# A mixture-of-experts stage whose tiles are weighted at the gate and added in DRAM by an accumulating indirect transfer

## The chip, the cores and the metric

The kernel runs on one core of one Trainium2 chip. The metric is the device time of one execution in microseconds (us), median over runs. A core has five engines with instruction streams of their own: TensorE (PE in the profile; its weight loads are PEld), VectorE (DVE), ScalarE (ACT), GpSimd (POOL) and SyncE (SP, which here only issues transfers). 16 DMA engines carry the transfers that SP, ACT and POOL issue.

## The reference

One layer of a decoder over 2048 prompt tokens and 64 sample tokens (8 x 8), 1024 channels: adaLN modulation, a state-space branch beside windowed attention, an output projection with residual (x2), and a mixture of experts. The part that is changed:

```python
def hier_moe(x, ...):          # top-1 of 4 groups, then top-2 of its 4 experts
    wts = g_p * top_p / jnp.sum(top_p, axis=-1, keepdims=True)
    eid = g_idx[:, None] * EXPERTS_PER_GROUP + top_i
    gates = jnp.sum(jax.nn.one_hot(eid, N_EXPERTS) * wts[..., None], axis=1)
    hg, hu = einsum('td,edf->tef', xt, w_gate), einsum('td,edf->tef', xt, w_up)
    act = jax.nn.silu(hg) * hu * gates[..., None]
    return jnp.einsum('tef,efd->td', act, w_down)
...
ffn = hier_moe(hn2, ...)       # hn2: normed and modulated x2
x = x + gt2 * rms_norm(ffn, p['g_post_ffn'])
```

So each token has two experts, each with a weight; the two weighted outputs are summed, the sum is normed, and x2 is added. An expert has gate and up weights of 1024x256 each and down weights of 256x1024, in fp32. Products are computed in fp32 accuracy as three products of rounded and residual halves.

## The kernel before

The stages run one after the other: front, state space, attention, mixing, experts. The change touches the last two.

**Mixing** (function mixing) goes over 17 tiles of 128 tokens (NT = 17; the last has 64). SP loads inputs, and per tile stores the rows of x2 and of hn2 (the experts' input) to DRAM (L1716, L1717), then loads the next x (L1712).

**Experts** (function moe) has three parts.

The *plan*: DVE works out each token's two experts and their weights wts (from L2302 on), counts the rows of each expert, gives each expert whole tiles of 128 slots, 48 tiles in all (NTILE), and turns this into `rows` (for each slot the token whose row it takes, L2397) and `su` (for each token its two slots, L2394). `plan` holds per tile the expert, whether it differs from the tile before (fresh), and the buffer slot of its weights (expert's ordinal modulo NSL = 3).

The *loop* over 48 tiles, rolled in fours. SP issues the gate and up weights of tile t+2 (L2127) as soon as DVE has split the tile NSL earlier, and the down weights of tile t (L2132) once the down product of tile t-NSL is done; both transfer only where the tile is fresh. POOL gathers the rows of hn2 (L2169; four buffers x, refilled when PE has transposed one) and stores each output tile o (two buffers) to the scratch tensor moe (L2174). PE computes gate and up of tile t+1 (24 products of 128x512 into ps_h), transposes the rows of t+2 (L2510), then the down product of t (L116 to L118 and L2536 into ps_o), then transposes the gated activations of t+1. ACT takes the tanh (L2221), moves transposed rows (L2209) and rounds weights (L2213, L2231); DVE makes the gate (L2426, L2428), and the residual halves (L2403, L2409, L2416). Both copy one half of ps_o to o (L2239, L2433), which waits for the store of two tiles before. So the order of each engine is written out by hand, with semaphores between them.

The *end*: SP loads 14 of the 17 x2 tiles into the free weight buffers (L2148; three are kept from the start). After the last store POOL gathers, for each of 17 token tiles, two rows per token from moe (L2195, 34 transfers, four tiles ahead). ACT scales the first by its weight (L2279), DVE scales and adds the second (L2467), ACT sums squares (L2284) and takes the root (L2286), DVE inverts (L2472), multiplies by the norm and by the row G2 (L2474), adds x2 (L2480), and SP stores y (L2157). G2 holds the modulation times gain, one broadcast row for the prompt (L2151) and eight small pieces for the sample tokens (L2153). It lies in the buffer o, so it is loaded after the last store, and DVE waits for all nine before the first L2474.

## Time and profile before

| | us |
|---|---|
| median of 3 runs (lowest, highest) | 1721.35 (1715.22, 1725.27) |
| the profiled execution | 1717.71 |
| its span, first to last instruction | 1715.9 |

| engine | busy us, share of the span |
|---|---|
| PE | 1389.4 (81%) |
| PEld | 1068.6 (62%) |
| DVE | 1201.2 (70%) |
| ACT | 745.6 (43%) |
| POOL | 433.6 (25%) |

The shares are averages over stages that have different limits. In the profile, the loop over experts' tiles runs from about 1148 to 1621 us, the end from there to 1715.9. A row of the trace shows start, duration, engine, line, operation, output<-inputs, and in brackets how long the engine was idle before and what it waited for. Names of scratch tensors lose their digits: scratch_x is x2, scratch_hn is hn2.

### The profile page before, as it was taken

The numbers are of one execution on the slowest core, as the hardware profiler recorded it, in microseconds if no ns is written. First come the engines' busy times: TensorE is split into PE (matmuls) and PEld (weight loads), VectorE is DVE, ScalarE is ACT, GpSimd is POOL, SyncE is SP. The second block draws the span as 40 slices with busy tenths as digits, with TensorE's granted clock in tenths as the row PEclk, the third lists the DMA queues.
The fourth block names the chain that finished last, engine by engine and source line by source line (L and its number), as shares of the span: only waits on it lengthen the run. The fifth ranks groups of instructions, "written<-read, shape, count | busy, mean of one in ns | idle before, by whom it ended". The sixth has DMA issues, their size and how long they took to land. (4 is left out here: it accounts for less than half of the span.)

```text
span 1715.9 us, 24334 instructions
## 1 busy us (share of the span) xinstructions
PE 1389.4 (81%) x7010; PEld 1068.6 (62%) x7011; DVE 1201.2 (70%) x2157; ACT 745.6 (43%) x1564; POOL 433.6 (25%) x541
## 2 busy tenths in 40 slices
PE   3299989877896789679999999439999999999600
PEld 1188878664664556468878787327777777777400
DVE  2887898754664567546555555479899898989468
ACT  1222221202332648533333333127777777777354
POOL 2504346233221870012111111011111111110063
PEclk9599999987998889889998988659999999999955
DMA  9412344439996752203333222255667775752597
GB/s 287 131 68 74 116 170 166 165 146 312 338 314 194 191 183 76 90 25 109 112 108 110 99 98 74 96 185 175 208 235 250 257 242 195 263 192 86 207 360 297
DMA packets 147982, 300.38 MB, mean 175 GB/s; under 512 B 30172, under 2 KB 87797, under 8 KB 144430
## 3 DMA queue, kind: packets, MB, share of 16 engines
q1 hardware_dynamic: 113830, 215.94, 36.8%
q0 software_dynamic: 23328, 78.32, 12.9%
q10 hardware_dynamic: 10752, 5.24, 1.3%
q8 instruction: 35, 0.57, 0.1%
q14 instruction: 37, 0.30, 0.1%
HBM read 307.09 MB, written 94.10 MB: 234 GB/s over the span
## 5 line engine op out<-in xcount | busy, mean ns | idle before, releaser
L2409 DVE TENSOR_TENSOR ex_w_lo<-ex_wgu,ex_w_hi 128x1024 fp32r<-128x1024 f32 x192 | 226.1, 1220 | 12.7 <-ACT ex_w_hi L2213 11.9
L2213 ACT ACTIVATE ex_w_hi<-ex_wgu 128x1024 fp32r x192 | 191.9, 1054 | 20.6 <-DMA ex_wgu<-in_w_exp_up_dram 20.6
L116 PE MATMUL ex_ps_h<-ex_w_hi,ex_xT 128*128 128x512 f32 x384 | 155.4, 405 | 3.1 <-DVE ex_x_lo L2403 3.1
L118 PE MATMUL ex_ps_h<-ex_w_hi,ex_x_lo 128*128 128x512 f32 x384 | 151.1, 393 | 0.0
L117 PE MATMUL ex_ps_h<-ex_w_lo,ex_xT 128*128 128x512 f32 x384 | 150.2, 391 | 0.0
L116 PE MATMUL fr_ps_m<-fr_whi,fr_hl 128*128 128x512 f32 (+1 forms) x408 | 150.0, 368 | 0.0
L117 PE MATMUL fr_ps_m<-fr_wlo,fr_hl 128*128 128x512 f32 (+1 forms) x408 | 147.9, 363 | 0.0
L118 PE MATMUL fr_ps_m<-fr_whi,fr_hl 128*128 128x512 f32 (+1 forms) x408 | 147.4, 361 | 0.0
L116 PE MATMUL mx_ps_m<-mw_hi,mx_hT 128*128 128x512 f32 x272 | 107.2, 394 | 2.0 <-DVE mx_h_lo L1865 2.0
L1751 POOL TENSOR_SCALAR mx_st<-mx_st 128x1 f32<-128x1 f32 x68 | 29.4, 433 | 308.9 <-ACT mx_j L1795 189.7
L118 PE MATMUL mx_ps_m<-mw_hi,mx_h_lo 128*128 128x512 f32 x272 | 106.9, 393 | 0.0
L117 PE MATMUL mx_ps_m<-mw_lo,mx_hT 128*128 128x512 f32 x272 | 106.8, 393 | 0.0
L2169 POOL DMA_INDIRECT ex_x<-scratch_hn,ex_rows x48 | 47.6, 993 | 203.6 <-PE ex_ps_t L2510 167.7
L2536 PE MATMUL ex_ps_o<-ex_wd,ex_aT 128*128 x192 | 97.9, 592 | 0.0
L116 PEld LDWEIGHTS fr_ps_m<-fr_whi,fr_hl 128*128 128x128 f32 x408 | 79.4, 195 | 14.7 <-issue 3.1
L2174 POOL DMA_DIRECT2D scratch_moe<-ex_o x48 | 27.5, 574 | 238.0 <-DVE ex_o L2433 238.0
L118 PEld LDWEIGHTS fr_ps_m<-fr_whi,fr_hl 128*128 128x128 f32 x408 | 79.3, 194 | 11.7
L117 PEld LDWEIGHTS fr_ps_m<-fr_wlo,fr_hl 128*128 128x128 f32 x408 | 79.3, 194 | 11.4
L116 PEld LDWEIGHTS ex_ps_h<-ex_w_hi,ex_xT 128*128 128x128 f32 x384 | 72.5, 189 | 17.4 <-DVE ex_x_lo L2403 2.4
L118 PEld LDWEIGHTS ex_ps_h<-ex_w_hi,ex_x_lo 128*128 128x128 f32 x384 | 72.4, 189 | 16.4
L117 PEld LDWEIGHTS ex_ps_h<-ex_w_lo,ex_xT 128*128 128x128 f32 x384 | 72.8, 189 | 14.0
L404 ACT ACTIVATE fr_hl<-fr_ps_t 128x512 fp32r<-128x512 f32 x34 | 18.5, 595 | 135.3 <-PE fr_ps_t L470 135.3
(430 smaller groups left out, 3448.7 us busy)
## 6 DMA issues: line engine op xcount, KB each, us to landing
ex_wgu<-in_w_exp_gate_dram SPq DMA_DIRECT2D x48, 1024.0 KB
ex_wgu<-in_w_exp_up_dram SPq DMA_DIRECT2D x48, 1024.0 KB
ex_wd<-in_w_exp_down_dram SPq DMA_DIRECT2D x48, 1024.0 KB
scratch_moe<-ex_o POOLq DMA_DIRECT2D x48, 512.0 KB
scratch_rec<-fr_w SPq DMA_DIRECT2D x16, 1112.0 KB, 5.9
s_rec<-scratch_rec SPq DMA_DIRECT2D x32, 556.0 KB, 7.1
s_w<-in_w_ada_dram SPq DMA_DIRECT2D x16, 1024.0 KB, 8.1
scratch_proj<-fr_io SPq DMA_DIRECT2D x17, 640.0 KB
```

Of the source, the lines that this page charges most:

```text
L116: nc.tensor.matmul(out, hi, w_hi, start=first, stop=False)
L117: nc.tensor.matmul(out, hi, w_lo, start=False, stop=False)
L118: return nc.tensor.matmul(out, lo, w_hi, start=False, stop=final)
L404: A(hi[:, t % 2, 4 * h:4 * h + 4, :], ps_t[:, h, :].rearrange("p (k n) -> p k n", k=4), ACT.Copy).then_inc(moved_a, 1)
L1751: last = nc.gpsimd.tensor_scalar(a[:, col + m:col + m + 1], a[:, col + m:col + m + 1], c, EPS, ALU.mult, ALU.add)
L2169: pool.indirect_dma_start(x[:, t % U, :], None, T["hn2"], bass.IndirectOffsetOnAxis(rows[:, t:t + 1], 0)).then_inc(S["x", t % U], 16)
L2174: pool.dma_start(T["moe"][t * P:(t + 1) * P, :], o[:, t % 2, :]).then_inc(sem("st", t % 2), 16)
L2213: A(w_hi[:, par, c * PW:(c + 1) * PW], wgu[:, bass.ds(slot * (KD * 2 * DE) + c * PW, PW)], ACT.Copy).then_inc(S["w_rounded"], 1)
L2409: vec.tensor_tensor(w_lo[:, par, c * PW:(c + 1) * PW], wgu[:, bass.ds(slot * (KD * 2 * DE) + c * PW, PW)], w_hi[:, par, c * PW:(c + 1) * P ...
L2536: last = nc.tensor.matmul(ps_o[:, at], aT[:, 1, :], wd[:, bass.ds((slot * 2 + 1) * D + c * 512, 512)], start=False, stop=True)
```

## The change

The kernel's output is the same; the two experts' rows of a token are now combined as the tiles are made.

- Mixing: 18 DRAM-to-DRAM transfers of 512 KB (clear) write zeros to a new scratch tensor acc (2304 rows of 1024), one behind each tile's stores on SP's queue, two at the end; the stage ends when they have landed. A row of hn2 in DRAM has 1028 elements instead of 1024.
- Plan: the two weights and two slots of each token (tail, 4 numbers) are written behind the rows of hn2 by one transfer that ACT issues, in pieces of 16 bytes (128 x 17 = 2176). The first gather waits for it. `rows` takes one DVE instruction more; `to` (each slot's token row in acc, or a spare row where the slot is empty) takes three, behind it. `su` goes.
- Loop: gathers bring 4112 bytes a row. POOL finds each row's weight by three small instructions a tile (weigh), and DVE's gate applies it (a tensor_tensor becomes a scalar_tensor_tensor). The store becomes an indirect transfer that adds the 128 rows of o to acc, and each waits until the one before has landed. Weight buffers go from three to two (NSL = 2); so the waits on SP are for a tile one later.
- End: no gathers from moe, no scaling, no sum. SP loads the 17 tiles of acc with plain transfers, 16 of them at once (NF = 16) on its one queue, with the broadcast G2 row behind the first and the eight small G2 pieces behind the sixteenth. 9 tiles of x2 are kept from the start (4.5 MB are loaded there instead of 1.5) and 8 loaded here instead of 14.

```diff
+            def clear(t):
+                sp.dma_start(accv[:, bass.ds(t, 1), :], zeros).then_inc(S["zeroed"], 16)
+
...
                     load_ya(after2)
                 if before:
                     store(before)
+                    clear(before.t)
                     if after:
                         load_x(after)
...
             store(Tile(0, LAST))
+            clear(LAST)
+            clear(NT)
+            sp.wait_ge(S["zeroed"], (NT + 1) * 16)
             for n in ("stx", "sth"):
...
-NSL = 3
+NSL = 2
 U = 4
-NKEPT = 3
+NKEPT = 9
+NF = 16
 AHEAD = 2
...
+        sd, st_, sp_ = (s.sb(n, [P, 2 * NT]) for n in ("sd", "stau", "srow"))
+        tail = s.sb("tail", [P, NT, 4])
+        wts, sf = (tail[:, :, 2 * n:2 * n + 2].rearrange("p t k -> p k t") for n in range(2))
+        rowf, none, rows, to = s.sb("rowf", [P, NTILE]), s.sb("none", [P, NTILE]), s.sb("rows", [P, NTILE], U32), s.sb("to", [P, NTILE], U32)
+        eq2, wt2, wt = s.sb("eq2", [P, 2]), s.sb("wt2", [P, 2]), s.sb("wt", [P, U])
         ones1, et, plan, et_n = s.sb("ones1", [1, NTILE]), s.sb("et", [1, 3, NTILE]), s.sb("plan", [1, 3, NTILE], I32), s.sb("et_n", [1, NTILE])
...
-        f = wgu[:, 2 * U * D:3 * U * D].rearrange("p (n d) -> p n d", n=U)
-        f1, g = wd[:, 0:3 * D].rearrange("p (n d) -> p n d", n=3), wd[:, 3 * D:5 * D].rearrange("p (n d) -> p n d", n=2)
-        y, junk = x, wd[:, 5 * D:6 * D]
-        names = ("x2_in G2_in eps_set f1_ready f_ready summed rooted rstd g_ready y_ready loaded step de exped hot counted planned matched turned rows_ready x_flipped x_moved_a x_moved_v w_rounded w_split x2_rest d_rounded d_split a_split gu_done th_ready "
+        f_of = lambda t: wgu[:, t % NF * D:(t % NF + 1) * D] if t % NF < 8 else spare_lo[:, t % NF - 8, :]
...
             sp.wait_ge(S["st_odd"], (HT + 1) * 16)
+            def load_f(t):
+                R = rows_of(t)
+                sp.dma_start(f_of(t)[R, :], T["acc"][t * P:t * P + R.stop, :]).then_inc(S["f", t % NF], 16)
+
+            load_f(0)
             sp.dma_start(G2[:, 0, :], mod_row(T, 5)).then_inc(S["G2_in"], 16)
+            for t in range(1, NF):
+                load_f(t)
             for b in range(DB):
                 sp.dma_start(G2[b * DT:(b + 1) * DT, 1, :], mod_row(T, 5, 1 + b, DT)).then_inc(S["G2_in"], 16)
             for t in range(NT):
                 sp.wait_ge(S["y_ready"], t + 1)
                 dst = T["o_y_sample"].rearrange("b t d -> (b t) d") if t == LAST else yv[:, t, :]
                 sp.dma_start(dst, y[rows_of(t), t % U, :]).then_inc(S["y", t % U], 16)
+                if t + NF < NT:
+                    sp.wait_ge(S["g_ready"], t + 1)
+                    load_f(t + NF)
             for n in range(U):
...
             pool.dma_start(free[0:16, 2:4], T["rconst"][0:16, 2:4]).then_inc(S["st_odd"], 16)
+            pool.wait_ge(S["tail_out"], 16)
             pool.wait_ge(S["rows_ready"], 1)
+            chain = Steps(pool, S["weighed"])
+
+            def weigh(t):
+                n = t % U
+                pool.wait_ge(S["x", n], (t // U + 1) * 16)
+                chain.then(nc.gpsimd.tensor_scalar(eq2[:, :], x[:, n, D + 2:], C["place"][:, t:t + 1], None, ALU.is_equal))
+                chain.then(nc.gpsimd.tensor_tensor(wt2[:, :], eq2[:, :], x[:, n, D:D + 2], ALU.mult))
+                nc.gpsimd.tensor_tensor(wt[:, n:n + 1], wt2[:, 0:1], wt2[:, 1:2], ALU.add).then_inc(S["wt_ready"], 1)
 
             def gather(t):
...
                 pool.wait_ge(S["o_out_v"], t + 2)
-                pool.dma_start(T["moe"][t * P:(t + 1) * P, :], o[:, t % 2, :]).then_inc(sem("st", t % 2), 16)
+                if t:
+                    pool.wait_ge(sem("st", (t - 1) % 2), ((t - 1) // 2 + 2) * 16)
+                pool.indirect_dma_start(T["acc"], bass.IndirectOffsetOnAxis(to[:, t:t + 1], 0), o[:, t % 2, :], None, compute_op=ALU.add).then_inc(sem("st", t % 2), 16)
...
             for t in range(U):
                 gather(t)
-            refill(0)
-            refill(1)
+            for t in range(2):
+                weigh(t)
+                refill(t)
+            pool.wait_ge(S["to_ready"], 1)
             for t in range(NTILE):
+                if t + 2 < NTILE:
+                    weigh(t + 2)
                 if t + 2 < NTILE - U:
                     refill(t + 2)
                 store(t)
             pool.wait_ge(S["st_even"], (HT + 1) * 16)
             pool.wait_ge(S["st_odd"], (HT + 1) * 16)
-
-            for t in range(NT):
-                if t >= U:
-                    pool.wait_ge(S["f_ready"], t - U + 1)
-                for k in range(2):
-                    pool.indirect_dma_start(r[:, t % U, k, :], None, T["moe"], bass.IndirectOffsetOnAxis(su[:, k, t:t + 1], 0)).then_inc(S["r", t % U], 16)
...
+            act.wait_ge(S["tailed"], 1)
+            act.dma_start(T["hn2"].rearrange("(n p) d -> p n d", p=P)[:, :, D:], tail[:, :, :]).then_inc(S["tail_out"], 16)
...
             round_d(NTILE - 1, U - 1, NTILE // U - 1, slot_of(NTILE - 1))
             out(NTILE - 1, 1, HT - 1)
 
-            def first(t):
-                R = rows_of(t)
-                act.wait_ge(S["r", t % U], (t // U + 1) * 32)
-                if t >= 3:
-                    act.wait_ge(S["f_ready"], t - 2)
-                A(f1[R, t % 3, :], r[R, t % U, 0, :], ACT.Copy, scale=wts[R, 0, t:t + 1]).then_inc(S["f1_ready"], 1)
-
             def root(t):
                 R = rows_of(t)
-                act.wait_ge(S["f_ready"], t + 1)
-                A(junk[R, :], f[R, t % U, :], ACT.Square, accum_out=norm[R, t, 0:1]).then_inc(S["summed"], 1)
+                act.wait_ge(S["f", t % NF], (t // NF + 1) * 16)
+                A(junk[R, :], f_of(t)[R, :], ACT.Square, accum_out=norm[R, t, 0:1]).then_inc(S["summed"], 1)
                 act.wait_ge(S["summed"], t + 1)
                 A(norm[R, t, 1:2], norm[R, t, 0:1], ACT.Sqrt, scale=1.0 / D, bias=eps[R, :]).then_inc(S["rooted"], 1)
 
             act.wait_ge(S["eps_set"], 1)
-            first(0)
-            first(1)
             for t in range(NT):
                 root(t)
-                if t + 2 < NT:
-                    first(t + 2)
 
...
             tt(slot[:, :, :], sumt[:, :, :].rearrange("p e t -> p t e"), ps_r.rearrange("p (t e) -> p t e", t=NT), ALU.add)
             tt(prod[:, :, :, :], OH[:, :, :, :], slot[:, :, :].unsqueeze(1).broadcast_to([P, 2, NT, NE]), ALU.mult)
-            red(sf[:, :].rearrange("p (k t) -> p k t", k=2), prod[:, :, :, :], ALU.add)
-            tt(sd[:, :], sf[:, :], C["dump"], ALU.add)
+            red(sf, prod[:, :, :, :], ALU.add)
...
                 ts(Tq[:, h, 0, :], Tq[:, h, 0, :], C["q"], None, ALU.mult, ALU.bypass)
                 vec.tensor_tensor(Pm[:, h, :], sp_[:, h].unsqueeze(2).broadcast_to(wide_p), C["iota"].unsqueeze(1).broadcast_to(wide_p), ALU.is_equal).then_inc(S["matched"], 1)
                 dve.wait_ge(S["matched"], n + 1)
-            chain.mark(vec.tensor_copy(su[:, :, :].rearrange("p k t -> p (k t)"), sf[:, :]))
             dve.wait_ge(S["turned"], 1)
             chain.then(vec.tensor_copy(rowf[:, :], ps_i[:, NTILE:]))
-            vec.scalar_tensor_tensor(rows[:, :], rowf[:, :], float(P), ps_i[:, 0:NTILE], ALU.mult, ALU.add).then_inc(S["rows_ready"], 1)
+            chain.then(vec.scalar_tensor_tensor(rowf[:, :], rowf[:, :], float(P), ps_i[:, 0:NTILE], ALU.mult, ALU.add))
+            vec.tensor_scalar(rows[:, :], rowf[:, :], -1.0, 0.0, ALU.add, ALU.max).then_inc(S["rows_ready"], 1)
+            ts(none[:, :], rowf[:, :], 0.0, None, ALU.is_equal, ALU.bypass)
+            chain.then(vec.scalar_tensor_tensor(none[:, :], none[:, :], C["nowhere"], rowf[:, :], ALU.mult, ALU.add))
+            vec.tensor_scalar(to[:, :], none[:, :], -1.0, None, ALU.add).then_inc(S["to_ready"], 1)
 
...
+            def gate(t, n):
+                par = n % 2
                 dve.wait_ge(S["th_ready"], t + 1)
                 vec.scalar_tensor_tensor(sg[:, :], th[:, :], 1.0, ps_h[:, par, 0:DE], ALU.add, ALU.mult).then_inc(S["sg_ready"], 1)
                 dve.wait_ge(S["sg_ready"], t + 1)
-                vec.tensor_tensor(a[:, :], sg[:, :], ps_h[:, par, DE:], ALU.mult).then_inc(S["a_ready"], 1)
+                dve.wait_ge(S["wt_ready"], t + 1)
+                vec.scalar_tensor_tensor(a[:, :], sg[:, :], wt[:, n:n + 1], ps_h[:, par, DE:], ALU.mult, ALU.mult).then_inc(S["a_ready"], 1)
 
...
             split_d(NTILE - 1, slot_of(NTILE - 1))
             out(NTILE - 1, 1, HT - 1)
-
-            def weigh(t):
-                R = rows_of(t)
-                dve.wait_ge(S["f1_ready"], t + 1)
-                vec.scalar_tensor_tensor(f[R, t % U, :], r[R, t % U, 1, :], wts[R, 1, t:t + 1], f1[R, t % 3, :], ALU.mult, ALU.add).then_inc(S["f_ready"], 1)
 
             def finish(t):
                 R = rows_of(t)
                 dve.wait_ge(S["rooted"], t + 1)
                 vec.reciprocal(norm[R, t, 2:3], norm[R, t, 1:2]).then_inc(S["rstd"], 1)
                 dve.wait_ge(S["rstd"], t + 1)
-                vec.scalar_tensor_tensor(g[R, t % 2, :], f[R, t % U, :], norm[R, t, 2:3], G2[R, 1 if t == LAST else 0, :], ALU.mult, ALU.mult).then_inc(S["g_ready"], 1)
+                vec.scalar_tensor_tensor(g[R, t % 2, :], f_of(t)[R, :], norm[R, t, 2:3], G2[R, 1 if t == LAST else 0, :], ALU.mult, ALU.mult).then_inc(S["g_ready"], 1)
...
             dve.wait_ge(S["x2_in"], 16)
-            weigh(0)
-            weigh(1)
             dve.wait_ge(S["G2_in"], (1 + DB) * 16)
             for t in range(NT):
-                if t + 2 < NT:
-                    weigh(t + 2)
                 finish(t)
...
 SCRATCH = {"mods": ((1 + DB, 6, D), F32), "smods": ((P, 2, D), F32), "proj": ((TOK, INW), F32), "rec": ((NG, P, RECW), F32),
            "hpre": ((P, NG * DB), F32), "r8": ((P, NG), F32), "y": ((TOK, SW), F32), "bias_rows": ((P, RB), F32),
-           "attn": ((TOK, AW), F32), "attn_s": ((P, 2 * NKV * HD), F32), "x2": ((TOK, D), F32), "hn2": ((TOK, D), F32), "moe": ((NSLOT, D), F32)}
+           "attn": ((TOK, AW), F32), "attn_s": ((P, 2 * NKV * HD), F32), "x2": ((TOK, D), F32), "hn2": ((TOK, D + 4), F32), "acc": ((TOK + P, D), F32)}
 
```

How the instructions stand. POOL before, around the end of the loop: gathers of rows and plain stores alternate, then stores alone, and the 34 gathers from moe.

```order
L2169 DMA ex_x<-scratch_hn,ex_rows 128x1024
L2174 DMA scratch_moe<-ex_o 128x1024
L2169 DMA ex_x<-scratch_hn,ex_rows 128x1024
L2174 DMA scratch_moe<-ex_o 128x1024 x7
L2195 DMA ex_wgu<-scratch_moe,kept_su 128x1024 x34
```

POOL now, at the same place: ex_o is stored to scratch_acc, and the three small instructions of a later tile stand ahead of each store.

```order
L2201 DMA ex_x<-scratch_hn,ex_rows 128x1028
L2208 DMA scratch_acc<-ex_o,ex_to 2304x1024
L2196 TENSOR_SCALAR ex_eq<-ex_x,ex_rc 128x2
L2197 TENSOR_TENSOR ex_wt<-ex_eq,ex_x 128x2
L2198 TENSOR_TENSOR ex_wt<-ex_wt 128x1
L2208 DMA scratch_acc<-ex_o,ex_to 2304x1024
```

144 small instructions have come between the transfers; the 34 gathers at the end are gone, and nothing stands in their place.

SP before, behind the last weights: x2 tiles, the G2 row, its eight pieces, the outputs.

```order
L2148 DMA ex_w_hi<-scratch_x 128x1024 x8
L2148 DMA ex_w_lo<-scratch_x 128x1024 x5
L2148 DMA ex_w_lo<-scratch_x 64x1024
L2151 DMA ex_o<-scratch_mods 128x1024
L2153 DMA ex_o<-scratch_mods 8x1024 x8
L2157 DMA out_y_prompt_dram<-ex_x 128x1024 x16
L2157 DMA out_y_sample_dram<-ex_x 64x1024
```

SP now, at the same place (scratch_acc is what the experts' rows were added to):

```order
L2161 DMA ex_w_hi<-scratch_x 128x1024 x7
L2161 DMA ex_w_hi<-scratch_x 64x1024
L2166 DMA ex_wgu<-scratch_acc 128x1024
L2169 DMA ex_o<-scratch_mods 128x1024
L2166 DMA ex_wgu<-scratch_acc 128x1024 x7
L2166 DMA ex_w_lo<-scratch_acc 128x1024 x8
L2173 DMA ex_o<-scratch_mods 8x1024 x8
L2177 DMA out_y_prompt_dram<-ex_x 128x1024
L2166 DMA ex_wgu<-scratch_acc 64x1024
L2177 DMA out_y_prompt_dram<-ex_x 128x1024 x15
L2177 DMA out_y_sample_dram<-ex_x 64x1024
```

The sixteen loads of 512 KB from acc stand between the G2 row and its eight pieces.

## Rows read from the trace of the kernel before

**Rows 1.** The page's slices of the span: busy tenths of PE and of DMA.
```profile
PE   3299989877896789679999999439999999999600
DMA  9412344439996752203333222255667775752597
```
**Rows 2.** Windows, the loop (length, engines' busy time, clock, DMA share, GB/s).
```profile
1163.50:1605.00 441.50, 441.50 (x2005) 336.18 (x2004) 396.03 (x501) 327.11 (x500) 66.53 (x87) 1.00 0.59 206
```
**Rows 3.** The chain that ended last (start, us, engine, what, line), its last part.
```profile
1621.36 6.79 DMA scratch_moe<-ex_o
...
1632.77 10.54 DMA ex_wgu<-scratch_moe,kept_su
...
1649.67 1.30 DVE ex_wd L2474
...
1652.21 1.20 DVE ex_wgu L2467
...
1656.07 1.19 DVE ex_wgu L2467
...
1706.21 1.30 DVE ex_wd L2474
...
1708.86 1.29 DVE ex_wd L2474
1710.17 1.22 DVE ex_x L2480
```
**Rows 4.** Timeline: a fresh expert's weights on SP, ACT's gate and rounding, a store.
```profile
1183.66 0.39 SPq L2127 DMA_DIRECT2D ex_wgu<-in_w_exp_gate_dram  x1
1184.27 0.41 SPq L2127 DMA_DIRECT2D ex_wgu<-in_w_exp_up_dram  x1
...
1183.35 0.39 ACT L2221 ACTIVATE ex_gates<-ex_ps_h 128x256 f32<-128x256 f32 x1 [1.82 <-PE ex_ps_h L118]
...
1193.05 0.39 ACT L2221 ACTIVATE ex_gates<-ex_ps_h 128x256 f32<-128x256 f32 x1 [1.85 <-PE ex_ps_h L118]
...
1194.89 2.00 ACT L2213 ACTIVATE ex_w_hi<-ex_wgu 128x1024 fp32r x2
...
1199.61 0.58 POOL L2174 DMA_DIRECT2D scratch_moe<-ex_o  x1 [4.47 <-DVE ex_o L2433]
```
**Rows 5.** Windows: a burst with fresh weights; one store alone.
```profile
1184.60:1194.00 9.40, 9.40 (x45) 7.13 (x44) 8.39 (x12) 6.84 (x12) 1.41 (x2) 1.00 0.97 332
...
1200.00:1202.10 2.10, 2.10 (x11) 1.71 (x11) 2.10 (x3) 0.93 (x1) 0.18 (x1) 1.00 0.63 252
```
**Rows 6.** Windows: the end, while x2 tiles are loaded.
```profile
1611.00:1634.20 23.20, 5.78 (x19) 3.02 (x17) 3.32 (x5) 2.52 (x5) 5.10 (x7) 0.74 1.01 370
1619.00:1631.00 12.00, 1.09 (x4) 0.22 (x2) 0.69 (x1) 0.60 (x1) 2.28 (x3) 0.64 1.02 415
```
**Rows 7.** Line L2148 (14 loads of x2 tiles): issues, time to landing.
```profile
L2148 SPq DMA_DIRECT2D ex_w_lo<-scratch_x x6: 447/473/797, 1614.0 to 1616.6; - x6
...
DMA to landing us min/median/max: 3.4/10.9/17.6
```
**Rows 8.** Timeline: the end of mixing.
```profile
1095.68 0.43 SPq L1717 DMA_DIRECT2D scratch_hn<-mx_hn  x1
...
1101.74 0.18 DVE L1902 COPY kept_lg<-mx_ps_t 128x20 f32<-128x20 f32 x1 [3.71 <-PE mx_ps_t L1993]
```
**Rows 9.** Timeline: the plan's slots, and the first gather.
```profile
1126.50 0.20 DVE L2302 TENSOR_TENSOR ex_sd<-ex_sf,ex_rc 128x34 f32<-128x34 f32 x1
...
1139.74 1.06 POOL L2169 DMA_INDIRECT ex_x<-scratch_hn,ex_rows  x1 [34.64 <-DVE ex_rows L2397]
```
**Rows 10.** DMA issues by line (KB, median us to landing): 16-byte rows.
```profile
mw_w_rt<-in_w_group_router_dram POOLq DMA_DIRECT2D x1, 16.0 KB, 7.6
```
**Rows 11.** The page's groups: small POOL instructions (busy, mean ns, idle before).
```profile
L1751 POOL TENSOR_SCALAR mx_st<-mx_st 128x1 f32<-128x1 f32 x68 | 29.4, 433 | 308.9 <-ACT mx_j L1795 189.7
```
**Rows 12.** Groups on ACT from 1652 us: the sum of squares.
```profile
L2284 ACT ACTIVATE ex_wd<-ex_wgu 128x1024 f32<-128x1024 f32 (+1 forms) x14 | 14.8, 1057 | 8.4 <-DVE ex_wgu L2467 8.2
```

More of the change, by code:

```diff
@@ L1659, in mixing @@
                  "z_ready z_flipped z_hi z_moved glu_done glu_used th2_ready o_ready ss5 ss34 p3 r34 hc_ready hc_part h_flipped h_moved_a h_moved_v mix_done "
-                 "ss1 p1 r1 mix_used x2_ready ss2 p2 r2 hn_part hn_ready n_flipped n_moved_a n_moved_v routed lg_used passed halved scaled").split()
+                 "ss1 p1 r1 mix_used x2_ready ss2 p2 r2 hn_part hn_ready n_flipped n_moved_a n_moved_v routed lg_used passed zeroed halved scaled").split()
         S = {n: s.sem(n) for n in names}
@@ L1687, in mixing @@
         tiles = lambda a: a.rearrange("(n p) d -> p n d", p=P)
-        yv, av, x2v, hnv = tiles(T["y"]), tiles(T["attn"]), tiles(T["x2"]), tiles(T["hn2"])
+        yv, av, x2v, hnv = tiles(T["y"]), tiles(T["attn"]), tiles(T["x2"]), tiles(T["hn2"])[:, :, 0:D]
         xp = T["x_prompt"].rearrange("a (n p) d -> p (a n) d", p=P)
         xs = T["x_sample"].rearrange("b t d -> (b t) d")
+        accv, zeros = tiles(T["acc"]), T["zeros"].unsqueeze(1)
         @blk.sync
@@ L2031 @@
 _at = 0
-for _n, _w in (("iota", P), ("tile", 2 * NT), ("order", 4), ("keep", NE * NT), ("q", 1), ("valid", NT), ("dump", 2 * NT), ("tau", NTILE)):
+for _n, _w in (("iota", P), ("tile", 2 * NT), ("order", 4), ("keep", NE * NT), ("q", 1), ("valid", NT), ("dump", 2 * NT), ("tau", NTILE), ("place", NTILE), ("nowhere", 1)):
     RC[_n] = (_at, _w)
@@ L2096, in moe @@
         for n in range(U):
-            for name in ("gu", "d", "x", "r", "y"):
+            for name in ("gu", "d", "x", "y"):
                 S[name, n] = s.sem(f"{name}{n}")
+        for n in range(NF):
+            S["f", n] = s.sem(f"f{n}")
         HT = NTILE // 2
@@ L2443, in step @@
                 own = slot_of(t)
-                gate(t, par)
+                gate(t, k % U)
                 move_x(t + 1)
@@ L2458, in _ @@
                 step(NTILE - U + k, k, NTILE // U - 1, k == 1)
-            gate(NTILE - 1, 1)
+            gate(NTILE - 1, U - 1)
             out(NTILE - 2, 0, HT - 1)
```

25 lines of the change are left out of this document (13 added, 12 removed).

## The prediction

> **What bounds the kernel now.** I read the page's slices first, then the windows of the loop, the chain, and the timelines of SP, POOL and ACT at three seams. The slices [rows 1] show PE at 9 tenths in the stretch of slices 27 to 37, and at 0 in the last two, where DMA is busy: two stages with different limits. In the loop PE is busy 441.50 of 441.50 us at the full granted clock [rows 2], one tile every 9.70 us (from one tanh to the next, 1183.35 and 1193.05, [rows 4]). DVE has 396.03 us of work there, about 1.0 us free a tile; the DMA engines are at 0.59. Behind the last store DVE sets the time: three large instructions a tile, one tile every 3.86 us (1652.21 to 1656.07, [rows 3]); only the last two tiles, which have no scaling left, take 2.65 us each (1706.21 to 1708.86). So there are three questions: does the loop stay at 9.70, what does the new end take, and what do the seams cost.
>
> **The end, before.** The last store is issued at 1621.36 and landed at 1628.15 [rows 3]. From there to the end of the span are 87.75 us. Of these, 21.5 pass before DVE's first multiplication at 1649.67 (the gathers land late, 10.54 us in the chain).
>
> **The end, now.** Call the landing of the last store T. The 34 gathers, 17 scalings on ACT and 17 on DVE go. DVE keeps 17 tiles at 2.65 us, 45.0 us. But it waits for all nine pieces of G2 before the first, and eight of them now stand on SP's queue behind sixteen loads of 512 KB. Does a later transfer of a queue wait for earlier ones? The 14 loads of x2 tell: issued one after the other, they land 3.4 us after issue at best and 17.6 at worst, the last issued at 1616.6 [rows 7], so at 1634.2, when all 7.1 MB are in. I take it that the small pieces wait too. Ahead of them are 17 transfers (16 tiles and the G2 row) of 0.524 MB, 8.9 MB. At 415 GB/s (1619 to 1631, [rows 6]) that is 21.5 us; with 2.1 us of start and landing (3.4 less the 1.3 of one tile's data) 23.6. At 370 GB/s (1611 to 1634.2, the same group) it is 26.2. DVE then starts at T+23.7, is through at T+68.7, and the last store to the end of the span takes 4.5 us, as now (1710.17+1.22 to 1715.9): T+73.2. ACT's squares (1.06 us each, [rows 12]) run ahead meanwhile and are hidden; without that cover the first would cost about 2. The seventeenth tile of acc is asked for once two tiles are through and has 40 us. Gain in the end: 87.75-73.2 = 14.5 us, with the slower rate 12.
>
> The Trainium skill (DMA: Bandwidth & Descriptors, "Queues, rings and completion order") says that on each DMA engine descriptors are consumed in ring order. This speaks against the change's order of loads: by it the sum is as above, and without it the second case below. The landing times of the x2 tiles agree with it.
>
> **T itself.** The last store now reads its target as well, and waits for the one before it; on the other hand 8 x2 tiles compete, not 14: 4.2 MB at 370 GB/s from 1611 are in by 1622.4 and not at 1634.2. Bounds: 2 us earlier, 5 later (the 6.79 less the issue, nearly doubled). I take 0.
>
> **The accumulating stores in the loop.** No row shows one. Below, it is a plain store: issued 1199.61 [rows 4], data moved until 1202.1, 0.63 of 2.1 us [rows 5], landed 2.5 us after issue. Above, it takes twice the last store's 6.79, 13.6 us. Each waits for the one before, so the loop keeps its pace while landing plus POOL's issue of about 1 us stays under 9.70: up to 8.7 us. Where a store takes 13.6, the loss would be 4.9 us on 47 tiles, 230 us. I take 4 to 6 us (the nearest row is the 2.5 us store; a second read of 0.52 MB adds 1.3 to 2.1), under the threshold: 0. A single late store harms nothing, since o has two buffers.
>
> The Trainium skill (Collectives: The Full Stack, "The bandwidth ceiling: the fold count and why AG ≠ RS ≠ AR") has an adding transfer push two reads through the same ring and measures 1.93 times the time. By it the 2.1 us of data would be 4.1, an estimate, and the loop's sum stays at 0. No row here shows an adding transfer.
>
> **Weights: two slots.** The gate and up weights for tile t+2 are now asked for at the split of tile t, one tile later: at G+0.3, with G the tanh of tile t-1, and needed by ACT's rounding at G+11.54 (1194.89 in the terms of [rows 4]: 1183.66 would be the issue). The burst with such an issue, one gather and a plain store ran at 0.97 of the engines until about 1194.0, 9.4 us at 332 GB/s [rows 5], 3.1 MB. The second read adds 0.52 MB, 1.6 us: 1195.6, 0.7 late if the weights are the last to land. DVE's 1.0 us of free time takes that. The down weights come one tile later too; where experts change after two tiles they add 1.05 MB to a burst, 3.2 us, and are needed some 15 us after G, not 11.5. I take 0. The upper bound has the down weights ahead as well: 1198.8, 3.9 late, less 1.0 of DVE's and 1.1 before PE needs it, 1.8 us for each of the 14 experts whose weights are fetched inside the loop: 25 us. If all lands as before, the cost is nothing, and no gain is to be had since PE never waited.
>
> **POOL and DVE in the loop.** Three small instructions a tile at 0.43 us [rows 11], 1.3 us and some waits among them, and an indirect issue instead of a plain one (1.06 in [rows 9], 0.58 in [rows 4]): POOL is busy 66.53 of 441.50 us [rows 2] and would be at some 150. The weight is ready two tiles ahead of its gate. Behind the wait for the store before stand the next tile's weight and the refill, both with more than a tile in hand. The gate's new form is the same size. Gathers of 4112 bytes: 0.4% more data, hidden. Cost 0; if POOL's issue were 3 us longer, still 0.
>
> **The seams.** *Mixing's end.* The last stores are issued by 1095.68+0.43, DVE ends at 1101.92 [rows 8]. Two clears of 0.52 MB behind the stores: these landed about 3.5 us after issue, at 1099.2; then 1.3 us each at 415 GB/s is 1101.8, or 2.1 each at the lone store's rate 1103.4. Cost 0 to 1.5, I take 1.0. The sixteen clears before lie in a stretch where the DMA engines are mostly free (2 to 5 tenths, [rows 1]), and the loads behind them have a tile in hand: 0. *Plan.* The tail transfer can go out at 1126.5 and the first gather at 1139.74 [rows 9], 13.2 us of cover. 1024 pieces of 16 bytes took 7.6 us to land beside others [rows 10]; 2176 would take 16.2 if all of it scaled, 3 us too late, and about 8 if half was waiting. Cost 0 to 3, I take 0. One more DVE instruction of 0.2 us stands ahead of the first gather: 0.2 us. Keeping nine x2 tiles loads 4.7 MB at the start of the stage, 12.8 us at 370 GB/s, over before the slots are known at 1126.5: 0.
>
> **Sum.** -14.5 + 0 (T) + 0 (stores) + 0 (weights) + 1.0 + 0.2 = -13.3 us. On the profiled execution's own time, 1717.7 (span 1715.9), that is 1704.4. The median of the runs is 3.6 us above that execution, so I forecast 1721.35-13.3 = 1708.0. The own range, with T from -2 to +5, the slower rate (+2.6) and the seams at 0 to 4.7: 1704 to 1718.
>
> **Rivals.**
> *G2 gets through early, or its wait does not bind* (faster). For it: the pieces are small and on few partitions; against: the landing times of [rows 7]. Then DVE starts when the first tile is landed, squared and rooted, about T+6.3; it fills the four y buffers by T+17, then waits for the first y, whose store stands behind the loads, until T+23.7. 12 tiles and an addition are left, 33 us, plus 1 and 4.5: T+62.2. The gain is 25.5-1.2 = 24.3: 1697.
> *The weights come late* (no change). For it: the margin is 0.7 us on the wrong side, and the burst was at 0.97 already. Against: 1 us of slack on DVE, PE's own. At half the bound, 12.5 us, the gain is gone: 1720.5.
> *The adding store sets the tile's time* (slower). Place: POOL waits for the landing of store t-1 before issuing t. It decides from 8.7 us. For it: no row shows one, and the last store took 6.79 us in a full queue, bursts fill the queue in about a third of the loop. Against: the lone store's 2.5. At 1.5 times 6.79, 10.2 us, it costs 1.5 us on 47 tiles, 70 us: 1778.
> *The tail is late or acc is cleared late*: bounded above at 4.7 us, inside the own range.
>
> **How the numbers follow.** Forecast 0.52, G2 early 0.14, weights late 0.17, store bound 0.15, the rest is something unseen. What a measurement here can tell from no change is about 0.5%, 8.6 us, so faster means under 1712.7. Faster: 0.52 x 0.9 + 0.14 = 0.61; same: 0.05 of the forecast and 0.14 of the late weights, 0.19; slower: 0.15 and the worse part of the late weights, 0.20. The range takes in the forecast's own, the early G2 and the late weights up to no gain: 1694 to 1724, and leaves out the bound store.
>
> **What would show it.** In the new profile: tiles in the loop still 9.70 us apart, with POOL's idle time before a store ended by DVE's copy and not by a transfer (if by the store before: the third rival). ACT's rounding never waiting for a transfer from the weights (else the second). DVE idle before its first multiplication for about 24 us after the last store, ended by a transfer to ex_o; then 17 tiles at 2.65 us without a gap. The expert stage starting at most 1.5 us later, and the first gather released by DVE's rows, not by the tail. The prediction is wrong if the first multiplication starts within 10 us of T, or if the tile's distance rises anywhere.

## The result, and the profile after

The changed kernel is slower: 1739.93 us median of 4 runs (1738.56 to 1742.86) against 1722.4 of the kernel before, ratio 1.011 (95% interval 1.008 to 1.015), some 17.5 us. The forecast was 1708.0, and its range ended at 1724: the prediction was wrong. Of the profiled executions, before has 1717.7 us and the changed kernel 1742.9 (spans 1715.9 and 1741.0), 25.1 apart. The table places the difference. In the trace of before the first tanh is at 1155.25, the last at 1610.14 and T, the landing of the last store, at 1628.15 ([rows 3]); in the changed kernel they are at 1163.36, 1642.16 and 1663.55.

| distance, us | before | after | difference | forecast |
|---|---|---|---|---|
| start of the span to the first tanh of the expert loop | 1155.3 | 1163.4 | +8.1 | +1.2 |
| first tanh to the last (48 tiles) | 454.9 | 478.8 | **+23.9** | 0 |
| last tanh to T (landing of the last store) | 18.0 | 21.4 | +3.4 | 0 |
| T to the end of the span | 87.75 | 77.45 | **-10.3** | -14.5 |

Of the first 8.1 us, 6.0 are there at mixing's first load of y (719.97 before, 725.97 after), ahead of everything that the change touches in that stage, and 2.0 of them are given back in mixing; this is the difference of two executions (in the profiles of the twelve experiments below the first tanh is anywhere from 1153.8 to 1167.2). The medians differ by less than the two profiled executions, presumably for that reason among others. What is left is told under the seams.

The page's slices of the changed kernel, in tenths, answer to [rows 1]:

```profile
PE   3299989869986889679999999259999999999900
DMA  9422354449995752214333333467788877875574
```

PE has 9 in the loop here too, but the DMA engines stand at 7 and 8 where they had 5 to 7. The window over the loop answers to [rows 2] (columns as there):

```profile
1171.00:1640.00 469.00, 451.80 (x2021) 340.92 (x2020) 393.68 (x505) 325.11 (x502) 203.47 (x223) 0.99 0.73 194
```

PE now stands idle for 17.2 us of 469, and the DMA engines are busy 0.73 of the time instead of 0.59 while they move less per second, 194 GB/s instead of 206. Busier with less: that is the clue. (The profile counts the rows of an adding store once, as those of a plain one: 48.4 MB on POOL's queue in either case, below. What the addition reads back is not in its GB/s.) ACT's waits in the loop (engine, line, who was waited for, total us, times, longest):

```profile
ACT ex_w_hi L2245 <- DMA ex_wgu<-in_w_exp_up_dram: 30.1, 12, 6.4
ACT ex_w_hi L2245 <- issue: 14.2, 18, 1.3
ACT ex_wd_hi L2263 <- DMA ex_wd<-in_w_exp_down_dram: 12.3, 6, 2.7
```

No such wait on a transfer stood in the loop before. One of these stalls in the timeline, the tanh, the weights' issues, and the roundings that wait for them (answers to [rows 4]):

```profile
1491.23 0.38 ACT L2253 ACTIVATE ex_gates<-ex_ps_h 128x256 f32<-128x256 f32 x1 [0.47 <-PE ex_ps_h L118]
1501.75 0.38 ACT L2253 ACTIVATE ex_gates<-ex_ps_h 128x256 f32<-128x256 f32 x1 [2.63 <-PE ex_ps_h L118]
1506.10 2.01 ACT L2245 ACTIVATE ex_w_hi<-ex_wgu 128x1024 fp32r x2 [2.39 <-DMA ex_wgu<-in_w_exp_up_dram]
1511.33 1.06 ACT L2263 ACTIVATE ex_wd_hi<-ex_wd 128x1024 fp32r x1 [2.41 <-DMA ex_wd<-in_w_exp_down_dram]
1514.19 0.36 ACT L2253 ACTIVATE ex_gates<-ex_ps_h 128x256 f32<-128x256 f32 x1
...
1493.25 0.39 SPq L2140 DMA_DIRECT2D ex_wgu<-in_w_exp_gate_dram  x1
1493.85 0.78 SPq L2140 DMA_DIRECT2D ex_wgu<-in_w_exp_up_dram  x1
1497.33 1.48 SPq L2145 DMA_DIRECT2D ex_wd<-in_w_exp_down_dram  x1
```

From tanh to tanh these are 10.5 and 12.4 us instead of 9.70. The gate weights are asked for 2.0 us after the tanh (forecast: 0.3), the up weights land 12.2 us after their issue, and ACT wants them at 1503.7. Then the down weights are late as well, 13.9 us after issue. Of the 47 distances 13 are over 9.9 us; the others are 9.7 to 9.9 but for the first, 8.7 here and before.

The end. Columns of the first piece: the L2166 loads of acc from issue to landing (us, min/median/max); then issues on SP, DVE's first work after T = 1663.55, and three steps of the chain (start, us). They answer to [rows 3, 7].

```profile
DMA to landing us min/median/max: 3.3/10.2/16.4
...
1674.99 3.00 SPq L2173 DMA_DIRECT2D ex_o<-scratch_mods  x8
...
1691.24 0.16 DVE L2495 RECIPROCAL ex_norm<-ex_norm 128x1 f32<-128x1 f32 x1 [36.79 <-DMA ex_o<-scratch_mods]
1691.44 1.28 DVE L2497 SCALAR_TENSOR_TENSOR ex_wd<-ex_wgu,ex_norm,ex_o 128x1024 f32<-128x1024 f32 x1
...
1646.70 10.03 DMA scratch_acc<-ex_o,ex_to
1657.51 6.04 DMA scratch_acc<-ex_o,ex_to
1677.70 13.46 DMA ex_o<-scratch_mods
```

DVE's first multiplication starts 27.9 us after T, released by the last small piece of G2, as forecast, but 4.2 us later than forecast. The two last adding stores stand one behind the other in the chain, 10.0 and 6.0 us.

### The profile page after: what moved, and what is told of

It reads as the page before. It is cut to its first block and busy times, and to the rows that moved or that the text cites. A ratio compares the mean times of both kernels' runs of the same rounds, so it can differ in the third digit from the quotient of the medians.

```text
span 1741.0 us, 24449 instructions
## 1 busy us (share of the span) xinstructions
PE 1405.2 (81%) x7010; PEld 1077.2 (62%) x7011; DVE 1177.8 (68%) x2143; ACT 723.1 (42%) x1547; POOL 532.4 (31%) x651
## 5 line engine op out<-in xcount | busy, mean ns | idle before, releaser
L2208 POOL DMA_INDIRECT scratch_acc<-ex_o,ex_to x48 | 93.7, 1952 | 265.2 <-DVE ex_o L2461 244.3
L118 PEld LDWEIGHTS fr_ps_m<-fr_whi,fr_hl 128*128 128x128 f32 x408 | 78.9, 193 | 11.6
L117 PEld LDWEIGHTS fr_ps_m<-fr_wlo,fr_hl 128*128 128x128 f32 x408 | 79.0, 194 | 11.3
L116 PE MATMUL ex_ps_o<-ex_wd_hi,ex_a_hi 128*128 128x512 f32 x96 | 63.3, 659 | 15.7 <-issue 8.8
```

The lines of the kernel that those rows point to most:

```text
L116: nc.tensor.matmul(out, hi, w_hi, start=first, stop=False)
L117: nc.tensor.matmul(out, hi, w_lo, start=False, stop=False)
L118: return nc.tensor.matmul(out, lo, w_hi, start=False, stop=final)
L2208: pool.indirect_dma_start(T["acc"], bass.IndirectOffsetOnAxis(to[:, t:t + 1], 0), o[:, t % 2, :], None, compute_op=ALU.add).then_inc(sem(" ...
```

## The experiments

Each ran beside the kernel before, on the same chip; its ratio is to that, so times of different experiments are compared by their ratios. Two suspects lay in the loop: the second weight buffer less (A) and the adding stores (B), or the two together (C). T is taken as the first load of acc.

**e1: the kernel before, on two slots**

```diff
-NSL = 3
+NSL = 2
-        wgu, wd = s.sb("wgu", [P, NSL * KD * 2 * DE]), s.sb("wd", [P, NSL * 2 * D])
+        wgu, wd = s.sb("wgu", [P, 3 * KD * 2 * DE]), s.sb("wd", [P, 3 * 2 * D])
```

> The kernel before with its weight plan on two slots instead of three (the buffers keep their size, so nothing else moves). Theory A, the slots: the gate and up weights are asked for one tile later, about 1 us after the tanh of the tile before, and need 12 us to land where 11 are left; in the trace of the changed kernel 12 waits of ACT for them add to 30 us. Then the time from the first to the last tanh grows here too, from 454.9 us by 12 to 24, the sum is 1734 to 1746, and ACT's rounding of gate and up waits for the weights about as often. Theory B, the adding stores: what makes the weights late is the second read of each store; with plain stores two slots are enough. Then the loop stays within 4 us of 454.9 and the time is within 0.3% of before.

Measured: 1720.2 us, ratio 0.9997 (0.9979 to 1.0014). All 48 tanh stand 9.70 us apart but the first pair (10.3). Two lines of ACT's waits in the loop:

```profile
ACT ex_w_hi L2213 <- issue: 0.4, 1, 0.4
ACT ex_wd_hi L2231 <- DMA ex_wd<-in_w_exp_down_dram: 0.3, 1, 0.3
```

Two slots alone cost nothing. A falls; the small margin is enough while nothing takes it.

**e2: the changed kernel, on three slots**

```diff
-NSL = 2
+NSL = 3
-NKEPT = 9
+NKEPT = 3
```
(With it x2 tiles 11 to 16 lie in the free halves of w_lo, and acc tiles 12 to 15 in w_lo and wd.)

> The changed kernel with three weight slots again; three tiles of x2 are kept instead of nine, 14 are loaded behind the last gate and up product, and the 16 loads of acc go to the twelve, two and two places then free. Theory A: the 24 us in the loop go, the tile time is 9.70 throughout, first to last tanh 455 to 460; the end stays (T to the end of the span 77 to 79): 1740 less 19 to 24, that is 1716 to 1721. Theory B: the adding stores cost their 24 us with three slots as well, first to last tanh still 470 or more, 1735 to 1742. Theory C, both are needed: the result is as by A, and the kernel before with two slots shows no loss.

Measured: 1723.2 us, ratio 1.002 (0.9996 to 1.004). First to last tanh 456.7 us, no tile over 9.8 but the first pair (10.3, as in e1). So the adding stores alone cost the loop nothing either: B falls, C stands. The time is 2 us above the range that was expected for it. POOL did wait for its adding stores here, and no other engine for POOL:

```profile
POOL scratch_acc L2208 <- DVE ex_o L2461: 182.1, 35, 7.2
POOL scratch_acc L2208 <- DMA scratch_acc<-ex_o,ex_to: 69.1, 13, 9.1
```

Last tanh to T is 24.6 us, 3.2 more than with two slots, since 14 x2 tiles and not 8 are loaded beside the last two stores.

**e3: stores that overwrite**

```diff
-                pool.indirect_dma_start(T["acc"], bass.IndirectOffsetOnAxis(to[:, t:t + 1], 0), o[:, t % 2, :], None, compute_op=ALU.add).then_inc(sem("st", t % 2), 16)
+                pool.indirect_dma_start(T["acc"], bass.IndirectOffsetOnAxis(to[:, t:t + 1], 0), o[:, t % 2, :], None).then_inc(sem("st", t % 2), 16)
```

> The changed kernel (two slots) with indirect stores that overwrite instead of adding, so a token's row keeps only the expert stored last; the wait for the store before stays. Theory A: the stalls stay, first to last tanh 470 to 479, and only the last two stores are shorter, 1 to 3 us: 1735 to 1740. Theory B or C: the stalls go, first to last tanh 455 to 460, 1715 to 1721. The time of POOL's issue also tells whether its 2.0 us belong to the adding or to the indirect address: by the adding 1 us or less here.

Measured: 1713.5 us, ratio 0.9965 (0.9946 to 0.9984). First to last tanh 456.7, last tanh to T 17.6 instead of 21.4, no wait of ACT for weights. It is the adding, not the addresses or the wait for the store before. The time is 1.5 us below the range expected, and POOL's issue takes 1.4 us, between the 2.0 of the adding store and the 1 that was expected if all of it were the adding's.

**e4: no weights fetched**

```diff
-            tt(fresh[:, 1:], expert[:, 1:], expert[:, 0:NTILE - 1], ALU.not_equal)
+            chain.then(vec.memset(fresh[:, 1:], 0.0))
```

> The changed kernel with the weights of one expert for all tiles: no weights are fetched in the loop but the first, everything else (adding stores, waits between them, gathers) stays. It asks whether the adding stores hold the loop by themselves. Theories A and C: no, tiles 9.70 us apart throughout, first to last tanh 455 to 457, 1714 to 1718. Theory B: the landing of one adding store after another, or POOL's 2 us per issue, costs time without the weights, first to last tanh 462 or more.

Measured: 1719.4 us, ratio 0.9986 (0.9968 to 1.0004), first to last tanh 456.7: the adding stores and POOL's 2.0 us of issue do not hold the loop by themselves. (The time is 1.4 us above the range expected.)

e3 and e4 also give the adding store its price. The first fence has the stores of e3 (its issue in ns, min/median/max, and its landing in us); the second those of e4:

```profile
L2208 POOL DMA_INDIRECT scratch_acc<-ex_o,ex_to x48: 961/1418/1770, 1174.4 to 1628.0; - x48
...
DMA to landing us min/median/max: 3.3/3.8/7.8
```

```profile
L2208 POOL DMA_INDIRECT scratch_acc<-ex_o,ex_to x48: 1557/2013/2052, 1174.7 to 1629.5; - x48
...
DMA to landing us min/median/max: 5.9/6.6/10.1
```

And here POOL's queue from 1150 to 1640 us, gathers and stores together (packets, MB, share of the 16 engines' time), of e3 and then of e4:

```profile
q0 software_dynamic: 13309, 48.52, 26.8%
```

```profile
q0 software_dynamic: 13275, 48.39, 47.3%
```

The same 48.4 MB take 20.5% of 490 us more, 100 us in 48 stores: **2.1 us of all 16 DMA engines per adding store on top of some 1.3** for a plain one, so 3.4. The 1.3 are from a window of e3 in which the 0.52 MB of a store move alone (length, engines, clock, DMA share, GB/s), 0.59 of 2.2 us:

```profile
1467.00:1469.20 2.20, 2.20 (x15) 1.92 (x15) 1.65 (x3) 0.56 (x2) 1.51 (x3) 1.00 0.59 238
```

The store's own packets, counted by their 4096 bytes in both traces from 1190 to 1580 us, give the same: 3.4 us of 16 engines for 128 of them in e4, 1.3 in e3. In e4 an adding store without weights beside it, and before its gather, has these two windows, its start and its further course:

```profile
1468.50:1470.50 2.00, 2.00 (x14) 1.59 (x12) 1.97 (x4) 1.44 (x3) 1.69 (x4) 1.00 0.81 82
1470.50:1472.00 1.50, 1.50 (x6) 0.89 (x5) 0.79 (x2) 0.74 (x1) 0.61 (x1) 1.00 1.05 208
```

At the start the engines are busy and move 82 GB/s: the first sixteen packets of a store take 0.9 us each (median over the stores of e4 in that stretch; 0.17 in e3). Afterwards it is 208 GB/s, with a median of 328 ns a packet; one of e3's takes 161 ns. In the stall shown above, the first 5 us of the burst read so in the changed kernel, and in e3 at the same tile so:

```profile
1492.20:1497.20 5.00, 4.41 (x17) 2.77 (x16) 4.38 (x7) 4.85 (x9) 2.22 (x4) 1.00 0.92 168
```

```profile
1468.40:1473.40 5.00, 5.00 (x24) 3.51 (x23) 4.39 (x6) 4.36 (x9) 1.23 (x3) 1.00 0.73 238
```

With the adding store 0.84 MB are counted in these 5 us, without it 1.19. The packets of the two traces at this expert, by their sizes, show what holds what up (us from the issue of the gate weights):

| data move | e3, overwriting | the changed kernel |
|---|---|---|
| store of the tile before | -1.2 to 0.2 | -0.6 to 3.3 |
| gate and up weights | 1.1 to 9.3 | 2.4 to 11.6 |
| down weights | 8.7 to 12.2 | 9.8 to 17.5 |
| next store | 11.3 to 13.1 | 11.3 to 15.7 |

The first adding store is still moving when the gate weights are asked for, and the next one moves beside the down weights. The overwriting one is through 0.2 us after they are.

**e7: ACT reads its slot numbers before the tanh** (two slots)

```diff
             def step(t, k, i, more=True):
                 par = k % 2
+                own = read_slot(t)
+                if more:
+                    slot = read_slot(t + 2)
                 gate(t, par)
                 move_x(t + 1)
...
```

> The changed kernel (two slots) in which ACT reads the slot numbers of a tile ahead of its tanh, not between the copy of x and the first rounding of the weights. With adding stores ACT stood idle there 0.8 us a tile with nothing in the profile to wait for (23.6 us in 31 tiles with three slots, 33.7 in 44 without weights), with overwriting stores 0.6 us in all. Theory: reading a register takes longer while an adding store moves its data, ACT's rounding and DVE's splitting move back with it, and the next expert's weights are asked for 1 us later. Then the idle time with no releaser goes, the weights are asked for at 0.3 to 0.6 us after the tanh instead of 1.1 to 2.0, and each of the 12 waits of ACT for them shrinks by about 1 us: first to last tanh 462 to 470, 1726 to 1732. Rival: the idle time is not the read, it stays, and the time is 1736 to 1742.

Measured: 1739.6 us, ratio 1.0095 (1.0057 to 1.0133); first to last tanh 477.3. Half of the theory holds: the idle time without a releaser is gone from ACT's waits (in the changed kernel 14.2 us in 18 tiles), so it was the register read. The gain did not come, and the time is in the rival's range although its reason is not the one found. ACT's waits in this kernel:

```profile
ACT ex_w_hi L2245 <- DMA ex_wgu<-in_w_exp_up_dram: 26.6, 13, 6.9
ACT ex_wd_hi L2266 <- DMA ex_wd<-in_w_exp_down_dram: 11.3, 5, 3.0
```

At the same expert as above the gate weights are asked for 1.5 us after the tanh instead of 2.0, ACT waits 2.08 us for them instead of 2.39, and then 3.05 instead of 2.41 for the down weights, 5.13 in place of 4.80. They are landed 18.2 us after the first issue here and 18.0 in the changed kernel. The burst as a whole is too long; moving its first part forward half a microsecond only passes the wait on. At the first two experts fetched in the loop the gate weights are asked for 0.3 us after the tanh here, as early as before, and ACT still waits for them, 0.35 and 0.76 us (in the changed kernel 1.1 and 1.4 us after it, and 2.24 and 1.46). That is the burst's own share.

**e5: G2 early** (two slots)

```diff
-        x2_kept, G2 = s.sb("x2", [P, NKEPT, D]), o
+        G2 = [v[:, :, :].rearrange("p k n -> p (k n)").bitcast(F32) for v in (xT, x_lo)]
...
             sp.wait_ge(S["gu_done"], NTILE)
+            sp.dma_start(G2[0][:, :], mod_row(T, 5)).then_inc(S["G2_in"], 16)
+            for b in range(DB):
+                sp.dma_start(G2[1][b * DT:(b + 1) * DT, :], mod_row(T, 5, 1 + b, DT)).then_inc(S["G2_in"], 16)
```

> The changed kernel with the G2 row and its eight small pieces loaded into the two buffers of the flipped x, behind the last gate and up product and ahead of the x2 tiles, instead of behind the loads of acc. Theory: DVE's first multiplication at T+27.9 waited for the last small piece, which stood on SP's queue behind 16 tiles. Then it starts at T+5 to T+8 now; the first y store is behind the 16 loads, so DVE waits at the fifth tile until about T+24, and 13 tiles of 2.65 us and 4.5 us are left: T to the end of the span 63 instead of 77.45, the time 1740-14 = 1726. Rival: the tiles of acc themselves come in slowly, so the first multiplication is at T+15 or later and the end keeps more than 70 us: 1733 or more. The loop is not touched: first to last tanh 476 to 481.

Measured: 1730.7 us (1717.8 to 1743.2 in 5 runs), ratio 1.007 (1.002 to 1.012). First multiplication at T+6.8, T to the end 62.5. DVE's waits at the end:

```profile
DVE ex_norm L2495 <- ACT ex_norm L2313: 17.4, 1, 17.4
DVE ex_x L2503 <- DMA out_y_prompt_dram<-ex_x: 6.2, 1, 6.2
```

The theory holds to half a microsecond: the wait for G2 is gone and the one for y's buffer behind 16 loads has taken its place. The median gained 9.3, not 14, and its interval overlaps that of the changed kernel (1.008 to 1.015), so the gain is shown by the profile's end and not by the medians. The runs are wide, and the profiled one is their fastest; its loop took 474.0 us, with 19 tiles over 9.9, and how much a two-slot loop varies from run to run was not settled.

**e6, e8 and e9: three slots, G2 early, and the queue of the y stores** (SP's, POOL's, ACT's)

```diff
-                sp.dma_start(dst, y[rows_of(t), t % U, :]).then_inc(S["y", t % U], 16)
+                act.dma_start(dst, y[rows_of(t), t % U, :]).then_inc(S["y", t % U], 16)
```

> Three weight slots and the early G2 together. If the two losses are separate they add: 1723 less 14, that is 1709, first to last tanh 456.7 and T to the end 63. If G2's early transfers ahead of 14 x2 tiles delay the last two stores, T comes 1 to 3 us later: 1710 to 1712.

> As the one before it, with the stores of y issued by POOL on its own queue, so they do not stand behind the 16 loads of acc. Theory: nothing then holds DVE between its first multiplication at T+6 and the end: 17 tiles of 2.65 us and 4.5 us, T to the end 56, the time 1702. Rival: the loads take the whole of the DMA engines' rate until T+22 whatever queue the stores are on, the first y lands late all the same and the end is 60 to 63: 1706 to 1709.

> Three weight slots, the early G2, and the stores of y issued by ACT on its own queue. With SP's queue DVE stood still for 5.3 us at the sixth tile, with POOL's it ran without a gap but the span ended 11 us after the last issue. Theory: ACT's queue has neither; first multiplication at T+10, 42.5 us to the last one, then 2.5 and a store of about 3 us: T to the end 58 to 60 (64.7 on SP's queue), the time 1712-5 = 1707. Rival: the late landing of the last store is not POOL's but that of any second queue; then T to the end is 64 or more and the time 1711 to 1715.

| | time | ratio | last tanh to T | first mult. | T to end |
|---|---|---|---|---|---|
| e6, SP | 1712.4 | 0.996 (0.993 to 0.998) | 25.9 | T+9.8 | 64.7 |
| e8, POOL | 1714.6 | 0.996 (0.994 to 0.998) | 25.7 | T+11.3 | 67.5 |
| e9, ACT | 1704.3 | 0.990 (0.987 to 0.993) | 25.7 | T+11.2 | 60.8 |

The expectation for e8 was missed. DVE does run without a gap, 17 tiles of 2.65 us, but after the last issue on POOL (1700.09) the end of the span is 11 us off. Two windows of it:

```profile
1701.00:1703.00 2.00, 0.00 (x0) 0.00 (x0) 0.00 (x0) 0.00 (x0) 0.00 (x0) 0.50 0.59 131
...
1703.00:1711.00 8.00, 0.00 (x0) 0.00 (x0) 0.00 (x0) 0.00 (x0) 0.00 (x0) 0.50 0.00 0
```

The data are through by 1703, and 8 us follow in which nothing in the profile moves. The time was expected at 1702, by the rival at 1706 to 1709. On ACT's queue (e9) it is 4.6 us from DVE's last result to the end. So it is POOL's queue and not any second one; why, the profile does not show.

**e10, e11 and e12: the x2 tiles, and the clears.** e10 loads eight x2 tiles ahead of the last stores and six behind the loads of acc; e11 also issues the last two clears ahead of the mixing loop; e12 puts the six between the loads of acc:

```diff
             for t in range(NF):
+                if t >= NKEPT + 8:
+                    load_x2(t, "f", t % NF)
                 load_f(t)
```

> As the one before it, with eight of the fourteen x2 tiles loaded ahead of the last stores and six behind the loads of acc. Theory: the 14 transfers of x2 beside the last two adding stores are what moved T from 21.4 to 25.9 us after the last tanh, and they still slow the first acc tile (first multiplication T+9.8 instead of T+6.8). Now the last tanh to T is 21 to 22, the first multiplication at T+7, T to the end 54 to 57: last tanh to the end 77, the time 1701. Rival: six more transfers behind the loads, 22 in all, delay the first y's landing on ACT's queue beyond the fifth tile, DVE stops there for some us, and what was won is given back: 1705 to 1709.

> As the one before it, with the last two clears of acc issued ahead of the mixing loop instead of at its end. The expert stage began 9.8 us after the last mixing store in the changed kernel, 8.2 before. Theory: that difference of 1.6 us goes and nothing else moves: 1699.5. Rival: the stage's beginning is not set by the clears, the distance stays at 9.8 us or more, 1701.

> As the one before it, with the six late x2 tiles issued each ahead of its tile of acc, the 12th to 17th, and not behind all sixteen. With them behind, DVE stood 8.8 to 10 us at the 12th tile, waiting for the last x2. Theory: it was the order, not the amount; the 12th tile of acc and of x2 are the 24th transfer, in by T+36 when DVE asks at T+6.8+11 x 2.65 = T+36. Then DVE stops for 0 to 3 us, T to the end 55 to 59 (65 to 66 with them behind), 1699 to 1701, 6 us under the two before. Rival: the amount of data decides, 40 tiles of 0.52 MB at 405 GB/s take 52 us whatever their order, the stops only spread over several tiles and T to the end stays 62 or more: 1703 to 1706.

e10: 1705.9 us, ratio 0.989 (0.986 to 0.992), no gain on e9's 0.990. Last tanh to T 22.4 and first multiplication at T+6.6, about as expected; but T to the end is 65.0, the rival's side, at the twelfth tile rather than the fifth:

```profile
DVE ex_x L2515 <- DMA ex_w_lo<-scratch_x: 8.8, 1, 8.8
```

e11: 1706.5 us, ratio 0.989 (0.987 to 0.992). From the last issue of a mixing tile's store to the expert stage's first it is 7.8 us again, as before, from 9.4 to 9.5 where the clears stood between:

```profile
1099.50 0.43 SPq L1721 DMA_DIRECT2D scratch_hn<-mx_hn  x1
1107.33 0.34 SPq L2125 DMA_DIRECT2D ex_rc<-in_rconst_dram  x1
```

So the clears took the 1.6 us. That is below what the medians tell: 1706.5 against 1705.9, where 1699.5 was expected.

e12: **1696.0 us, ratio 0.987 (0.984 to 0.990)**, faster than both kernels; 23.4 us under the runs of before beside it. T to the end 57.8, first multiplication at T+7.2; one stop of 0.9 us at the 16th tile is left. Of the end's 65 us it was the order that cost, not the amount. By their intervals the ratios of e9 to e12 are not apart.

## Why the prediction was wrong, step by step

- **The end.** Right in kind: DVE starts late because G2's small pieces are behind 16 loads, then 17 tiles at 2.65 us. Expected T+23.7 and 73.2, measured T+27.9 and 77.4. The rate was the mis-sized part: 415 GB/s was taken from a stretch in full flow, but the loads begin from rest (238 GB/s at 0.76 in the first 3 us, 300 in the next 3), and the eight pieces, issued over 3.0 us, land last. The rival with G2 early, as a mechanism of the unchanged order, is out; e5 made it by moving the pieces and got its T+62.2 (62.5).
- **T itself.** Taken as 0, bound +5; measured +3.4, e3 puts 3.8 on the adding. Two stores that may not overlap each pay the long landing beside x2's loads, 10.0 and 6.0 us in the chain; the prediction did not add the two.
- **The adding stores in the loop.** The landing was taken as 4 to 6 us, it is 6.6 at the median (e4), under the threshold of 8.7: e2 and e4 have 9.70 a tile. The 2.5 us that the prediction gave a plain store's landing are the end of its data; the plain stores of e1 land 3.8 us after issue at the median. The rival that the store sets the tile's time is out. The Trainium skill (Collectives: The Full Stack, "The bandwidth ceiling: the fold count and why AG ≠ RS ≠ AR") holds that the addition costs nothing but the second read, a factor of 1.93. Here a packet in full flow takes 328 ns against 161, 2.04 times, which is near it; with the slow first packets the DMA engines' time of a whole store grows from 1.3 to 3.4 us, 2.6 times. The measurement decides, and for the whole store the page's factor falls short.
- **Weights on two slots.** This is the step that failed. The prediction computed a landing 0.7 us late and took it as absorbed by DVE's 1.0 us. Its "second read, 1.6 us" of data is 2.1 us of engine time. The burst has part of two such stores in it, and only one was counted: the store of the tile before is still moving for 3 us after the gate weights are asked for, where an overwriting one is through (the table under e3 and e4). The 14 issues of gate weights come at G+0.3 to G+2.6, 11 of them at G+0.9 or later, not at G+0.3 (e3: G+0.3 to G+0.5): ACT's register read takes 0.8 us longer while an adding store moves, and issues as late as G+2.2 are left in e7 where that read is out of the way, behind tiles that had waited already. And the down weights, counted only in the upper bound, bind too. Measured: 12 waits for gate and up and 6 for down, 42 us of ACT's time, 23.9 us on the loop, just under the bound of 25. The rival "weights late" had the right mechanism, taken at half its bound.
- **POOL and DVE in the loop.** Right: no wait on POOL's weights, though an adding issue takes 2.0 us and not 1.06 and POOL is busy 203 of 469 us.
- **The seams.** Mixing's end +1.6 (taken 1.0, bound 1.5), shown by e11. The plan's tail was hidden, the first gather was released by DVE's rows: from the stage's start to the first gather 36.2 us before, 37.3 after. The first tanh is 1.4 us later still, behind the gathers; that was not followed up.

What failed in the sum was adding up margins. Two terms, each rightly zero by itself (e1, e2), draw on the same 1 us of slack.

## What to carry to other kernels

Where two edits are each free because of slack, ask whether it is the same slack: here a buffer less used up the margin of a transfer, and the adding store then lengthened the burst that it stands in. An adding transfer is to be priced in the DMA engines' time and not in bytes, and a load in a shared queue goes in the order in which its consumer asks, small vital pieces first.

## What the runs showed of the hardware

- An adding indirect store of 128 rows of 4 KB takes 3.4 us of all 16 DMA engines (e4), overwriting 1.3 (e3): the first sixteen packets 0.9 us each at the median against 0.17, all of them 328 ns at the median against 161. It lands 6.6 us after issue, 3.8 overwriting; its issue on POOL is 2.0 us, 1.4 overwriting, 0.58 for a plain direct one ([rows 4]).
- While such a store moves its data, a register read on ACT takes some 0.8 us longer (e2: 24 us in 31 tiles, in all of which a store was moving, and none in the 14 where none was; e7: gone when read elsewhere). That it takes an adding store is not shown: in e3, with 0.6 us in all, the stores were through before the read in 39 of 47 tiles.
- A kernel whose last stores are on POOL's queue ended 8 us after their data had moved (e8); on ACT's queue it ended 4.6 us after DVE's last result (e9).
